# Gate scatter products of an expert-retrieval kernel: from one f32 product a token to three bf16 products, with rows made token by token

## The reference, cut to what matters

```python
s1, i1 = lax.top_k(s[:, :, 0], PEER_TOPK)          # 16 best of 128 first keys, per token and head
s2, i2 = lax.top_k(s[:, :, 1], PEER_TOPK)          # 16 best of 128 second keys
cand = s1[..., :, None] + s2[..., None, :]
best, pos = lax.top_k(cand, PEER_TOPK)             # 16 experts per token and head
idx = take_along_axis(i1 * 128 + i2, pos)          # numbers in 0..16383
gate = softmax(best)
act = einsum('td,thkd->thk', h, expert_u[idx])
out = einsum('thk,thkd->td', gate * gelu(act), expert_v[idx])
```

## Time and profile before

| | |
|---|---|
| median of 3 runs | 4406.88 us (4405.5 to 4407.66) |
| time of the profiled execution | 4405.72 us |
| its span in the trace | 4404.0 us |
| granted TensorE clock, mean | 0.992 |
| PE busy | 4309.3 us, 98% |
| DVE busy | 1962.0 us, 45% |
| ACT busy | 1282.0 us, 29% |
| POOL busy | 2411.8 us, 55% |
| expert columns with gate steps | about 2330 to 3240 us from the span's start |

### The profile page before, as it was taken

The page is one execution under the profiler, slowest core; times in us unless marked ns, Lnnn a source line. Parts: engine busy times, 40 slices in busy tenths (PEclk is TensorE's granted clock), DMA queues, the critical chain, the costliest instruction groups (busy, mean ns, idle before and its releaser), DMA issues.

```text
span 4404.0 us, 52634 instructions
## 1 busy us (share of the span) xinstructions
PE 4309.3 (98%) x20777; PEld 3709.8 (84%) x20777; DVE 1962.0 (45%) x2352; ACT 1282.0 (29%) x1105; POOL 2411.8 (55%) x702
## 2 busy tenths in 40 slices
PE   7999999999999999999999999999999999999997
PEld 6888888777787887878999999999997777777776
DVE  1010035111112022038935777777736666666663
ACT  3222221233222122132343333333332222222222
POOL 3444443333343433433556777777767777777773
PEclk9999999999999999999999999999999999999999
DMA  4233322222223333222346888888887787878773
GB/s 153 96 120 124 119 93 95 86 86 76 86 87 130 120 111 115 96 77 86 130 146 252 305 307 316 307 309 314 308 302 284 305 319 302 307 308 311 313 291 114
DMA packets 201727, 859.52 MB, mean 195 GB/s; under 512 B 16784, under 2 KB 98768, under 8 KB 111312
## 3 DMA queue, kind: packets, MB, share of 16 engines
q1 hardware_dynamic: 62928, 458.26, 28.7%
q0 software_dynamic: 36864, 268.45, 15.6%
q10 hardware_dynamic: 101888, 132.23, 8.5%
HBM read 795.96 MB, written 62.91 MB: 195 GB/s over the span
## 4 chain that ended last, share of the span: by engine, by line
PE 94%; POOL 2%; DVE 2%; DMA 1%; ACT 1%; issue 1%; ACTq 0%; DVEq 0%
PE bank L1407 17%; PE bank L1408 17%; PE bank L1409 17%; PE bank L1429 16%; PE bank L1657 7%; PE bank L1661 7%; PE bank L1659 7%; POOL low L452 2%; PE bank L1633 2%; DVE wide L1310 1%; PE wide L1454 0%; DMA bs<-b_s 0%; PE wide L1544 0%; PE wide L1552 0%; POOL fetched L469 0%
## 5 line engine op out<-in xcount | busy, mean ns | idle before, releaser
L452 POOL TENSOR_TENSOR low<-raw,high 128x2048 fp32r<-128x2048 f32 x433 | 2049.9, 4734 | 1851.3 <-ACT high L509 1850.8
L509 ACT ACTIVATE high<-raw 128x2048 fp32r<-128x2048 f32 x433 | 829.9, 1917 | 2603.1 <-PE bank L1409 1477.9
L1407 PE MATMUL bank<-x_high,high 128*128 128x384 f32 (+1 forms) x3856 | 1398.3, 363 | 14.4 <-DVE x_low L1142 7.7
L1409 PE MATMUL bank<-x_high,low 128*128 128x384 f32 (+1 forms) x3856 | 1390.3, 361 | 0.0
L1408 PE MATMUL bank<-x_low,high 128*128 128x384 f32 (+1 forms) x3856 | 1389.9, 360 | 0.0
L1407 PEld LDWEIGHTS bank<-x_high,high 128*128 128x128 f32 x3856 | 725.4, 188 | 86.9 <-issue 8.3
L1409 PEld LDWEIGHTS bank<-x_high,low 128*128 128x128 f32 x3856 | 725.0, 188 | 71.2
L1408 PEld LDWEIGHTS bank<-x_low,high 128*128 128x128 f32 x3856 | 725.5, 188 | 69.9
L1657 PE MATMUL bank<-high,a_high 128*128 128x512 f32 x1536 | 609.5, 397 | 8.4 <-POOL low L452 8.4
L1661 PE MATMUL bank<-high,a_low 128*128 128x512 f32 x1536 | 608.0, 396 | 0.0
L1659 PE MATMUL bank<-low,a_high 128*128 128x512 f32 x1536 | 604.0, 393 | 0.0
(11 more groups left out here) (186 smaller groups left out, 2609.1 us busy)
## 6 DMA issues: line engine op xcount, KB each, us to landing
raw<-weights SPq DMA_DIRECT2D x433, 1024.0 KB, 4.8
act_dram<-act_out ACTq DMA_DIRECT2D x128, 192.0 KB
retrieved_dram<-stage ACTq DMA_DIRECT2D x48, 512.0 KB
act_in<-act_dram ACTq DMA_DIRECT2D x32, 768.0 KB
gates_in<-retrieved_dram ACTq DMA_DIRECT2D x32, 768.0 KB
gates_dram<-sgu_act ACTq DMA_DIRECT2D x32, 256.0 KB, 2.0
gate_in<-gates_dram ACTq DMA_DIRECT2D x32, 256.0 KB, 2.7
xa<-x SPq DMA_DIRECT2D x4, 1024.0 KB, 8.2
```

The source lines that it names most:

```text
L452: nc.gpsimd.tensor_tensor(low[:, slot, :], raw[:, slot, :], high[:, slot, :].bitcast(F32), ALU.subtract).then_inc(low_done, 1)
L509: nc.scalar.activation(high[:, slot, :], raw[:, slot, :], ACT.Copy).then_inc(high_done, 1)
L1407: nc.tensor.matmul(o, high[:, slot, w], x_high[:, 0:tiles, k, :], start=(k == 0), stop=False)
L1409: ins = nc.tensor.matmul(o, low[:, slot, w], x_high[:, 0:tiles, k, :], start=False, stop=(k == KT - 1))
```

## The change

The gate is split into three bf16 parts whose sum is the f32 gate: six instructions ahead of the first gate step. `rows` is now made for each part, and `hit2` (now `hit`) and `rows` are bf16. `hit1` is gone: each row is one `tensor_scalar` of 128x128 that compares the key numbers 0 to 127 (`iota`) with the token's key (a pointer scalar, one number per partition) and multiplies by the token's gate part (a second pointer scalar). PE does three products a token, accumulated in one bank. The buffers of `rows` and `hit` are single, and the waits stand where they stood.

```diff
-        hit1 = c("hit1", [P, WTOK, P])
-        rows = c("rows", [P, WTOK, P])
-        hit2 = c("hit2", [P, WTOK, P])
+        gate_part = c("gate_part", [P, 2, DENSE])
+        gate_bits = c("gate_bits", [P, DENSE], BF16)
+        hit = c("hit", [P, WTOK, P], BF16)
+        rows = c("rows", [P, 3, WTOK, P], BF16)
...
+            for part in range(2):
+                then(nc.vector.tensor_copy(gate_bits[:], gate_t[:]))
+                then(nc.vector.tensor_copy(gate_part[:, part, :], gate_bits[:]))
+                then(nc.vector.tensor_tensor(gate_t[:], gate_t[:], gate_part[:, part, :], ALU.subtract))
+            parts = [gate_part[:, 0, :], gate_part[:, 1, :], gate_t[:]]
...
                 dve.wait_ge(step_mm, steps.next())
-                then(nc.vector.tensor_tensor(hit1[:], keys, by_key(idx1_t, token), ALU.is_equal))
-                nc.vector.tensor_tensor(rows[:], hit1[:], by_key(gate_t, token), ALU.mult)
-                nc.vector.tensor_tensor(hit2[:], keys, by_key(idx2_t, token), ALU.is_equal).then_inc(rows_done, 1)
+                for n in range(WTOK):
+                    token = slice(first + n, first + n + 1)
+                    nc.vector.tensor_scalar(hit[:, n, :], iota[:], idx2_t[:, token], None, ALU.is_equal)
+                    for part in range(3):
+                        ins = nc.vector.tensor_scalar(rows[:, part, n, :], iota[:], idx1_t[:, token],
+                                                      parts[part][:, token], ALU.is_equal, ALU.mult)
+                ins.then_inc(rows_done, 1)
...
                     b, col = 2 + token // 4, token % 4 * P
-                    ins = nc.tensor.matmul(bank[b][:, col:col + P], hit2[:, token, :], rows[:, token, :], start=True,
-                                           stop=True)
+                    for part in range(3):
+                        ins = nc.tensor.matmul(bank[b][:, col:col + P], hit[:, token, :], rows[:, part, token, :],
+                                               start=(part == 0), stop=(part == 2))
```

More of the change, by code:

```diff
@@ L1275, in _, with gate_rows @@
             steps, taken = Count(), Count()
[L1277 to L1282, removed]
-                dve.wait_ge(step_mm, steps.next())
-                then(nc.vector.tensor_tensor(hit1[:], keys, by_key(idx1_t, token), ALU.is_equal))
-                nc.vector.tensor_tensor(rows[:], hit1[:], by_key(gate_t, token), ALU.mult)
-                nc.vector.tensor_tensor(hit2[:], keys, by_key(idx2_t, token), ALU.is_equal).then_inc(rows_done, 1)
+            for part in range(2):
[3 more added lines that the diff above has]
+            parts = [gate_part[:, 0, :], gate_part[:, 1, :], gate_t[:]]
+            def gate_rows(first):
+                dve.wait_ge(step_mm, steps.next())
+                for n in range(WTOK):
[5 more added lines that the diff above has]
+                ins.then_inc(rows_done, 1)
             def take():
```

## The result

The changed kernel takes 4435.56 us (median of 4 runs, 4433.97 to 4438.6), the kernel before 4406.35 in the same comparison. The ratio is 1.0067, with a 95% interval of 1.0049 to 1.0084: slower by 29 us. The forecast was slower, 4468 us, with a range of 4390 to 4560. The direction and the mechanism held; the size was twice too large.

A forecast was written before the change was run, and what follows sets the result against it. PE was taken to bound the gate steps, with DVE having 5.3 us to spare a turn. From 4405.7 us, -14 (products) + 70 (waits for DVE's rows) + 6 (start) = +62 gave 4468 us, range 4390 to 4560.

The forecast's parts named there:

- What bounds: Stretch of gate steps: PE is the bound, and DVE has 5.3 us to spare in a turn of 18.46 us.
- DVE's step undisturbed, 7.8 us: DVE's 32 instructions of a gate step, 0.20 us a hit and 0.26 a rows: 7.8 us, against 3.5 before.
- Held by POOL (55%): Gate steps: POOL's low parts stop DVE's new instructions, so DVE is late by 0.5 to 3 us a turn; 4468 us.
- The first rival: Gate steps: POOL does not hold DVE's small instructions, so their 9.9 us are hidden; 4396 us, chance 22%.
- The second rival: Gate steps: instructions held but about 0.05 us shorter, 6.2 us a step, PE waits nowhere; 4400 us, chance 5%.
- The third rival: Gate steps: DVE's back-to-back instructions keep POOL out, so PE waits 4.1 us a turn; 4594 us, chance 10%.
- PE's part, -14 us: PE's gate steps: 24 bf16 products take 1.5 us instead of 1.80, 0.3 us saved in each of 48 steps.
- The start, +6 us: First gate step: six more instructions and one low part inside the rows; the column follows at 2353.1 instead of 2346.90.
- The wait in the turns, +70 us: Gate-step turns: PE waits a mean 1.5 us for DVE's rows, 47 times; ends 0.5 (+24) and 4.9 (+230).
- the floor: PE's least wait for DVE's rows in a turn: 0.5 us, or 1.0 with three dots.
- its prices of 0.5, 1.0 and 2.1 us: PE's wait a turn: 0.5 us at the floor, 1.0 with three dots, 2.1 when POOL's fetch waits for a dot.
- The clock (8%): Gate-step turns: each wait slows PE's clock, a loss of about 2 us; near 4550 us, chance 8% alone.

The follow-up runs named there:

- odd counts: Changed kernel with key numbers in a padded tile, three rows of 43 (pitch 44), and 129 elements written for each row: 4396.7 us, ratio 0.9981.
- the two runs at 4576 and 4583 us: Changed kernel with POOL's fetches asked for one row later, 4576.0 us; changed kernel with one more DVE instruction a token, into an unread tile, 4582.65 us.

## Why the prediction was right in its course and wrong in its size

**What bounds.** Right. PE bounded the stretch of gate steps before, and DVE had 5.3 us to spare; after, DVE is idle 7.1 us in all between the second gate step and the last.

**DVE's step undisturbed, 7.8 us.** Right: 14.0 us less 1.7 and 4.5 of standing, and the instructions are 0.20 and 0.26 apart as worked out from the earlier trace rows. The six instructions ahead took 0.36 and 0.56 us each.

**Held by POOL (55%).** Right, and shown by two runs that change what the 32 instructions read, and how, with the same number of them: PSUM, and odd counts. The run with odd counts leaves the rest of the steps alone. The first rival, that these instructions are not held, is false for the shapes of the change, and true as soon as the counts are odd. That its time, 4396, is also what that version measured (4396.7) is partly luck: in the profiled execution of that run (4399.35 us) the turns gain 17 us, not 14, and the start costs 11, not 4. The second rival, shorter instructions, is false for the change (7.8 us a step), but its mechanism is what the bf16 key numbers bring about: 6.6 us a step and 4402.8 us, where it had 4400. The third rival, POOL starved, is false: its low part has a mean of 4665 ns.

**PE's part, -14 us.** Too small: 0.39 us a step, 19 us in 48. The products are 0.056 us apart, below my lower bound of 0.059. (The 0.067 of the prediction comes out with the interval unrounded, 8.33 / 48 = 0.1735 us, not with the 0.17 that it shows.) By the Trainium skill's 81 ns (TensorE: Matmul & The Clock Gate, "Back-to-back issue gap") the change would, as an estimate, have cost 7 us there; the trace does not agree, at 56 ns.

**The start, +6 us.** Too small: 10.2. I had one low part fall into the first rows. The timeline has two, one behind the other, L1291 held 5.52 us at 2338.82 and 5.58 us at 2344.72, since ACT had long rounded the next unit; PE waited 18.4 us and its clock was 0.64 over 2336 to 2358. The 4.64 us that PE waited for a low part before are gone, which is why 18.4 us cost only 10.

**The wait in the turns, +70 us: the step that failed.** "I take a mean wait of 1.5 us, between the floor and the turns with a late fetch" was a choice between 0.5 and 4.9, with no count behind it. It measured 0.79 a turn, 36 us in 46, of which 0.72 is waiting and the rest the lower clock in two turns. The cases of the prediction were all there, near its prices of 0.5, 1.0 and 2.1 us; what it lacked was how often each comes. The 46 turns of the changed kernel, sorted by the dots that DVE does ahead of the rows, and by whether a fetch of POOL had to wait over 1 us for a dot in that turn (a turn without a wait shows 0.16 us of idle time):

| turns | number | idle ahead of the weight loads, mean (range) |
|---|---|---|
| two dots, no such wait of POOL | 20 | 0.37 us (0.16 to 0.90) |
| three dots, no such wait of POOL | 15 | 0.76 us (0.31 to 1.14) |
| three dots, POOL waited 1.5 to 3.4 us | 11 | 1.94 us (1.06 to 2.73) |

One turn of the last kind, POOL's fetch behind a dot and PE's weight loads 18 us later:

```profile
2583.37 0.94 POOL L470 DMA_INDIRECT fetched<-expert_u,slot_i  x1 [3.00 <-DVE fetched L1304]
...
2601.09 2.21 PEld L1640 LDWEIGHTS bank<-rows,hit 128*128 128x128 bf16 x24 [2.24 <-DVE rows L1291]
```

With the prediction's own three prices these counts would have given an estimate of 1.05 us a turn, 49 us instead of 70. The rest is that the floor was lower: in the turn shown first, around 2839 us, DVE got 5.9 us of work in between the two low parts, where I had 5.6. The long waits are not just the turns with three dots, since 15 of these stay at 0.76. That a late fetch is their cause is read from this one trace, in which every wait of 2 us has such a fetch ahead of it; no run moved the fetches and left the rest alone.

**The clock (8%).** In the changed kernel it cost something at the start and 3 us in two turns, where the 24 products took 2.5 us instead of 1.5 (at 2601.09 and 3072.17). It is seen most in the two runs at 4576 and 4583 us, with a mean granted clock of 0.977 and 0.976 over the whole span.

Sum by the measured terms, over 46 turns: -18 for the products, +33 for the waits, +3 for the clock in two turns, +10 for the start, 28 of 28.2 us.

## What to carry to other kernels

An engine with 5 us to spare in a turn can take 4 us more of its own work and still be late, when what it adds are instructions that another engine's long instruction stops: count the longest hold as part of the turn. Where the sum of the two engines' exclusive times comes near the turn, a small change (1 us less or 2 us more of 18) moves the kernel by 33 or 147 us, so make the instructions of the kind that is not held, even when each gets longer. Look as closely at the first turn as at the steady ones: the same hold cost 10 us once there. Where the turns fall into cases of different price, work out how often each comes before you take a mean.

## What the runs showed of the hardware

- DVE `tensor_scalar` with f32 in and bf16 out is held by a POOL `tensor_tensor` for its whole length (5.08 us for a pair that takes 0.59 undisturbed), as f32 to f32 is (4.71 us instead of 0.34); between two DVE instructions that follow each other without a wait POOL gets in at once (2839.73 in the changed kernel).
- A source of three rows of 43 against a run of 129 takes a `tensor_scalar` out of that hold, at 0.32 us between instructions instead of 0.26; so does a source in PSUM, at the same pace.
- With key numbers and rows both in bf16 the same instructions are 0.16 and 0.22 us apart instead of 0.20 and 0.26, and still held.
- bf16 products of 128x128 with a weight load each are 0.056 us apart; f32 ones took two instructions of 0.112 each.
- Behind waits of 7 to 8 us of PE the next 24 products took 2.74 us instead of 1.51. Behind waits near 2 us they took 2.5 us in two turns and 1.51 in the others.
